# Row sums of an expert pair in one block, descriptor scratch cut to a quarter, and three quarters of weight unit 9 loaded into the place freed

## The chip, the cores and the metric

One core of one Trainium2 chip. The metric is the device time of one execution of the whole program in microseconds; where several executions are shown, their median counts. Profiles are of one execution; times in them are microseconds from the first instruction.

## The reference

One inference step of a one-layer encoder for a prompt of 512 rows and a sample of 32, model width 1024: an input projection `w_in` (8464 columns), an RWKV-7 branch and a chunked GLA branch, a gated merge, and a mixture of 32 experts (4 groups of 8, each token in the two best of its best group). The change is in the expert stage, and in what is loaded ahead of it:

```python
combine = jnp.sum(jax.nn.one_hot(expert_ids, N_EXPERTS, dtype=f32) * w_top[..., None], axis=1)
for e in range(N_EXPERTS):                       # D_MODEL 1024, EXPERT_FF 512, all float32
    hid = jax.nn.silu(ht @ e_gate[e]) * (ht @ e_up[e])
    out = out + combine[:, e:e + 1] * (hid @ e_down[e])
x = x + gt2 * out
y = _rmsnorm(x, final_norm_g)
```

Here `ht` are the normed rows of both streams, 544 in all, `gt2` a modulation from the condition `c` of the stream, and the outputs are `y` of both streams and the new states.

## The kernel before

The program has stages with their own semaphores and memory layout. The first makes the modulations and projects with `w_in` in 66 units of 128 columns; SyncE's queue loads them into two slots (L433), each load after the split of the unit two before (`w_split`). Beside the units 20 to 45 the GLA branch is computed for five tiles of rows. GpSimd (POOL) issues some DMAs in this stage: the GLA state (L513), and after each tile a store of its result `y_g` (`keep_y`, L521 to L525), each behind a wait on `y_g_out`, which VectorE raises twice per tile (L1162). VectorE waits for the five stores (`y_g_kept`) before it writes over that memory. The second stage is the recurrence. The third projects both branches with `w_branch_gla` and `w_branch_rwkv` in 16 units, called branches here: SyncE loads branch u + 2 (`load_branch`) once branch u is split (`wb_split`), and its gate rows (`load_gates`); ScalarE makes the high part of the weights (L1361, after the projection before the last is done), VectorE the rest (L1367), and TensorE multiplies (L2836). ScalarE's queue loads `w_out` and the residual rows beside branches 8 to 13. `gate_up_in` says that the small matrix `rwkv_gate_up` has landed. After a short output projection and the router comes the expert stage.

**The expert stage.** Experts are worked off in pairs p = 0 to 15, each expert for a block of up to 64 rows. The weights of an expert are three units of 2048 KB: gate, up, down. `STREAM` lists them per pair as gate 2p, up 2p, gate 2p+1, up 2p+1, down 2p, down 2p+1, so unit 9 is `up` 3. They go through a ring of eight slots (`RING`, `SLOT_AT`; one unit, `BESIDE`, has its own place). SyncE issues the loads in order (`load_unit`, L2155 to L2167; the DMA is at L2159 for whole units and at L2166 for quarters). A unit's slot is that of the ring unit eight before it; SyncE waits for TensorE to have read that one: `gu_mm` for a gate/up product, `dn_mm` for a down projection. Units 1 to 19 (`IN_QUARTERS`) are loaded in four quarters, each after the same quarter of the one before was read (`part_read`). `landed` tells the semaphore value for which TensorE waits.

Within a pair TensorE does, in order (L3131 to L3138):

- `gate_up(2p)`: for each of 8 slices k of the width, gate and up of the even expert into one bank (L3017). I call it product 2p. Before slice 6 it does `rows_added` of the pair before for tiles 0 and 1.
- `gate_up(2p+1)`: the same for the odd expert. Before slice 3 it turns the even product (`turned`, L3028) and does `rows_added` for tiles 2 and 3.
- `rows_turned(p+1)`: transposes the gathered rows of the next pair (L2991); `turned(2p+1)`.
- `rows_added(p-1, 4)`: the fifth tile.
- `down(p)`: both down projections (L3041), after VectorE's hidden rows (`hid_done`).

`rows_added(p, j)` (L3048 to L3063) brings the pair's results back to the places of their rows: a one-hot matrix times the result in two parts, 4 matmuls of 512 columns (L3061), into `ADD_BANKS[j]`: tiles 0 and 2 share banks 4 and 5, tiles 1 and 3 banks 6 and 7, tile 4 has banks 0 and 1, where the even product lies. VectorE adds each sum to the residual `x2` (`rows_summed`, L3529) and raises `moe_added`; the product for tile 2 waits for the sum of tile 0, that of tile 3 for tile 1. Banks 6 and 7 also take the turned rows, so `rows_turned` waits for the sum of tile 3, and `down` for that of tile 2. VectorE also copies products out (L3471), multiplies the hidden rows (L3464, after ScalarE's silu, L2704), scales the down result (L3497) and makes its two parts (ScalarE L2709, VectorE L3499). The last pair is done in another order (`held_rows`, `tile_so_far`, `last_rows`), and isn't touched.

POOL gathers the rows of the next pair with an indirect DMA (L2279) as soon as those of the present one are turned.

## Time and profile before

| | us |
|---|---|
| three runs | 1420.49, 1412.27, 1420.85 |
| median | 1420.49 |
| the profiled execution | 1418.71 |
| span of its trace | 1417.0 |
| TensorE busy in it | 1340.1 |
| VectorE, ScalarE, POOL busy | 704.2, 465.6, 173.3 |
| moved by DMA | 310.79 MB |

The span runs from the first to the last instruction; the execution's own time is 1.71 us longer. In the views PE is TensorE's matmuls, PEld its weight loads, DVE VectorE, ACT ScalarE, SPq and ACTq the DMA queues of SyncE and ScalarE. A wait stands behind the instruction that waited, as time and releaser. A DMA's landing is counted from its issue. "issue" is a wait for nothing that the profile shows. Matmuls are pipelined, so that the start of the next one tells more than the duration of one.

### The profile page before, as it was taken

Reading aid. Unit: us, or ns where it says so; the run is one execution under the profiler, and the core shown is the slowest. Engines: PE = TensorE matmul, PEld = TensorE weight load, DVE = VectorE, ACT = ScalarE, POOL = GpSimd, SP = SyncE. Lnnn points to the kernel's source line nnn. Section 1 sums busy time; section 2 is a strip of 40 time slices with the busy share of each in tenths; the row PEclk is TensorE's granted clock in tenths of the full one; section 3 lists DMA queues with packets and bytes.
Section 4 is the critical chain, followed back from the end, with each engine's and each line's share of the span. In section 5 each row is a group of like instructions: output and inputs, shape, how many; then the busy total and the mean of one; then the engine's idle time right before and its main releaser. Section 6 shows DMA issues by size and latency. Waiting matters only on the chain.

```text
span 1417.0 us, 30562 instructions
## 1 busy us (share of the span) xinstructions
PE 1340.1 (95%) x13401; PEld 986.4 (70%) x13401; DVE 704.2 (50%) x1139; ACT 465.6 (33%) x732; POOL 173.3 (12%) x212
## 2 busy tenths in 40 slices
PE   5899999999999997888889999999999999999997
PEld 1688899999999996777778998863444444343343
DVE  3413234553236556555576658634455544454454
ACT  2424235555665663343344343211100010000113
POOL 2000000000112213433430201000000000000000
PEclk9999999999999998999999999999999999999999
DMA  8566522224532210000052392899999999999993
GB/s 323 183 218 219 168 77 75 75 83 139 160 106 76 75 46 26 4 5 5 20 152 77 97 312 93 322 407 408 409 428 426 427 426 427 426 427 427 426 428 147
DMA packets 132932, 310.79 MB, mean 219 GB/s; under 512 B 13315, under 2 KB 98537, under 8 KB 119865
## 3 DMA queue, kind: packets, MB, share of 16 engines
q1 hardware_dynamic: 122078, 285.86, 53.9%
q10 hardware_dynamic: 7546, 15.58, 3.1%
q0 software_dynamic: 3168, 7.33, 1.4%
q8 instruction: 109, 1.79, 0.6%
q14 instruction: 31, 0.25, 0.1%
HBM read 299.88 MB, written 12.79 MB: 221 GB/s over the span
## 4 chain that ended last, share of the span: by engine, by line
PE 48%; DMA 7%; DVE 3%; issue 2%; ACT 1%; POOL 0%; SPq 0%; DVEq 0%; POOLq 0%; ACTq 0%
PE bank L3017 13%; PE bank L2836 7%; PE bank L3041 6%; DMA lower<-in_expert_w_up 4%; PE bank L3061 4%; PE bank L2864 3%; DMA upper7b<-in_expert_w_up 2%; PE bank L1761 2%; PE bank L1717 1%; PE bank L3028 1%; PE bank L2991 1%; PE bank L1818 1%; PE bank L1806 1%; PE bank L1793 1%; PE bank L2791 1%
## 5 line engine op out<-in xcount | busy, mean ns | idle before, releaser
L838 PE MATMUL bank<-upper2end 128*128 128x272 f32 x3168 | 416.7, 291 | 6.0 <-DVE upper2end L1065 5.4
L838 PEld LDWEIGHTS bank<-upper2end 128*128 128x128 f32 x3168 | 402.8, 189 | 26.9 <-issue 25.3
L3017 PE MATMUL bank<-upper7b 128*64 128x512 f32 x784 | 230.7, 596 | 7.6 <-issue 3.9
L1042 DVE TENSOR_TENSOR upper2end<-upper,upper2end 128x1024 fp32r<-128x1024 f32 x66 | 83.4, 1264 | 262.1 <-ACT upper2end L604 262.0
L3017 PEld LDWEIGHTS bank<-upper7b 128*64 128x64 f32 x784 | 69.8, 137 | 116.8 <-issue 116.5
L3017 PE MATMUL bank<-lower,upper7b 128*64 128x512 f32 x240 | 108.5, 596 | 2.4 <-issue 1.0
L3041 PE MATMUL bank<-upper7b,lower 128*64 128x512 f32 x352 | 106.3, 595 | 0.9 <-DVE lower L3464 0.9
L2836 PE MATMUL bank<-upper_r 128*128 128x272 f32 (+2 forms) x768 | 105.1, 293 | 0.0
L3529 DVE TENSOR_TENSOR lower<-lower,bank 128x1024 f32<-128x1024 f32 (+1 forms) x70 | 82.8, 1216 | 44.7 <-PE bank L3061 42.1
L2704 ACT ACTIVATE lower<-bank 128x256 f32<-128x256 f32 x32 | 12.3, 384 | 273.4 <-PE bank L3028 273.4
L2836 PEld LDWEIGHTS bank<-upper_r 128*128 128x128 f32 x768 | 98.2, 188 | 4.4 <-issue 0.9
L3061 PE MATMUL bank<-upper_r7b 128*128 128x512 f32 x280 | 75.3, 407 | 1.2 <-DVE upper_r7b L3499 1.2
L604 ACT ACTIVATE upper2end<-upper 128x1024 fp32r<-128x1024 f32 x66 | 69.6, 1054 | 17.0 <-DMA upper<-in_w_in 11.0
L3041 PEld LDWEIGHTS bank<-upper7b,lower 128*64 128x64 f32 x352 | 32.3, 137 | 49.4 <-issue 44.0
L2279 POOL DMA_INDIRECT lower<-expert_in,lower x16 | 16.0, 1000 | 398.5 <-PE bank L2991 388.4
L3061 PEld LDWEIGHTS bank<-upper_r7b 128*128 128x128 f32 x280 | 49.7, 190 | 21.2 <-issue 10.5
L2709 ACT ACTIVATE upper_r7b<-lower 128x1024 fp32r<-128x1024 f32 x15 | 15.9, 1057 | 127.3 <-DVE lower L3497 127.3
L3017 PEld LDWEIGHTS bank<-lower,upper7b 128*64 128x64 f32 x240 | 31.1, 137 | 33.2 <-issue 33.2
L3041 PE MATMUL bank<-lower 128*64 128x512 f32 x120 | 53.2, 595 | 0.0
L3471 DVE COPY lower<-bank 128x512 f32<-128x512 f32 x32 | 22.1, 692 | 60.9 <-PE bank L3017 60.9
L2864 PE MATMUL bank<-upper_r 128*128 128x512 f32 x192 | 45.8, 395 | 0.0
L1489 ACT ACTIVATE upper<-bank 128x512 f32<-128x512 f32 x36 | 21.5, 597 | 72.2 <-DVE upper L1574 72.0
(445 smaller groups left out, 1861.4 us busy)
## 6 DMA issues: line engine op xcount, KB each, us to landing
upper7b<-in_expert_w_gate SPq DMA_DIRECT2D x20, 2048.0 KB, 23.0
upper7b<-in_expert_w_up SPq DMA_DIRECT2D x19, 2048.0 KB, 28.3
upper7b<-in_expert_w_down SPq DMA_DIRECT2D x19, 2048.0 KB, 24.2
upper<-in_w_in SPq DMA_DIRECT2D x66, 512.0 KB, 3.9
lower<-in_w_ada SPq DMA_DIRECT2D x23, 1024.0 KB, 5.1
lower<-in_expert_w_down SPq DMA_DIRECT2D x7, 2048.0 KB, 25.0
lower<-in_expert_w_gate SPq DMA_DIRECT2D x6, 2048.0 KB, 21.9
lower<-in_expert_w_up SPq DMA_DIRECT2D x6, 2048.0 KB, 28.6
```

The costliest lines, as they stand in the source:

```text
L604: nc.scalar.activation(w_high[u % 2], w_slot[u % 2], ACT.Copy).then_inc(w_high_done, 1)
L838: m = mm(psum[s][:, c, 0:HALF], w_part[s][:, k, :], h_part[:, k, c * HALF:(c + 1) * HALF], start=k == 0 and w_part is w_high and h_part is ...
L1042: ve.tensor_tensor(w_rest[u % 2], w_slot[u % 2], w_high[u % 2].bitcast(F32), ALU.subtract).then_inc(w_split, 1)
L1489: nc.scalar.activation(kbv[c % 2][:, 2 * u:2 * u + 2].rearrange("p q h n -> p h q n"), psum[u % 2].rearrange("p h (q n) -> p h q n", n=256 ...
L1761: m = mm(out[r, j], lhs, pp[k % 2][r, j], start=True, stop=True)
L2836: m = mm(out, w[s][:, k, :], rhs, start=k == 0 and w is wb_high and y == "high", stop=k == KD - 1 and w is wb_rest)
L2864: m = mm(psum[OUT_BANKS[i]][:, 1 - b, :], m_part[side][:, k, t], w, start=k == first_k and m_part is m_high and w is not wo_rest[b][k], st ...
L3017: m = nc.tensor.matmul(GU_BANK[s][64 * b:64 * b + 64, :], x_t[:, k, s * BLK:(s + 1) * BLK], w[:, k, :], start=k == 0, stop=k == KD - 1)
L3041: m = nc.tensor.matmul(psum[2][64 * s:64 * s + 64, b, :], hid[s][:, f, :], down_rows(2 * p + s, f)[:, b * 512:(b + 1) * 512], start=f == 0 ...
L3061: m = nc.tensor.matmul(out[:, b, :], oh_t[:, j * P:(j + 1) * P], y_parts[part][:, b * 512:(b + 1) * 512], start=part == 0, stop=part == 1)
L3471: ve.tensor_copy(gu[e % 2], GU_BANK[e % 2]).then_inc(gu_out, 1)
L3529: ve.tensor_tensor(x2[0:n, j, :], x2[0:n, j, :], psum[ADD_BANKS[j]][0:n].rearrange("t b c -> t (b c)"), ALU.add).then_inc(moe_added, 1)
```

## The change

Four things. The scratch for POOL's descriptors is set to 4096 bytes, which leaves 12 KB per partition for a new tensor `apart`. Three quarters of unit 9 (`up` 3, slices 0 to 5) are loaded there, in three DMAs ahead of the load of branch 12, and TensorE reads these slices from there; only the last quarter still goes through the ring. The GLA state and the five stores of `y_g` are issued by SyncE instead of POOL, at units 22 and 28, 32, 36, 40, 44. And the five `rows_added` of a pair stand in one block in the odd product, before slice 3, in the order of tiles 0, 1, 4, 2, 3; VectorE's five sums likewise, after the hidden rows of the even expert.

```diff
+        apart = ctx.enter_context(nc.sbuf_tensor("apart", [P, 3 * D], F32)).rearrange("p (q k f) -> p q k f", q=3, k=2)
...
                 for u, (kind, f, col) in enumerate(UNITS):
+                    if u == 22:
+                        sp.wait_ge(b_sum, 2 * NG)
+                        sp.dma_start(st_g[1], I["state_gla"][0, 0].rearrange("h k v -> k h v")).then_inc(st_g_in, 16)
+                    if 28 <= u <= 44 and u % 4 == 0:
+                        i = (u - 28) // 4
+                        t0, wt = i * P, TILES[i][1]
+                        sp.wait_ge(y_g_out, 2 * i + 2)
+                        sp.dma_start(yg_dram[:, :, t0:t0 + wt].rearrange("n p t -> p n t"), y_g[:, :, t0:t0 + wt]
+                                     ).then_inc(y_g_kept, 16)
                     if u >= 2:
                         sp.wait_ge(w_split, u - 1)
...
-                pool.dma_start(st_g[1], I["state_gla"][0, 0].rearrange("h k v -> k h v")).then_inc(st_g_in, 16)
...
                     pool.tensor_tensor(q_st[:, :, 0:w], qk[:, 0:4, t], e_b[:, :, 0:w], ALU.mult).then_inc(q_st_done, 1)
-                    if i:
-                        keep_y(i - 1)
-                keep_y(4)
+                pool.wait_ge(y_g_out, 10)
...
-        gate_up_in = sem("gate_up_in", lasting=True)
+        apart_in = sem("apart_in", lasting=True)
...
+        APART = unit_no["up", 3]
...
         def parts_of(n):
-            return 4 if n in IN_QUARTERS else 1
+            return 4 if n in IN_QUARTERS and n != APART else 1
+        def load_apart(sp):
+            for q in range(3):
+                sp.dma_start(apart[:, q], eup[3][:, 2 * q:2 * q + 2]).then_inc(apart_in, 16)
+        def apart_landed(r):
+            return apart_in, r * 48 + 64
+        def block_rows(kind, e, k):
+            if unit_no[kind, e] == APART and k < 6:
+                return apart[:, k // 2, k % 2]
+            return weights_of(kind, e)[:, k, :]
...
+        ADD_ORDER = (0, 1, 4, 2, 3)
+        ADD_NO = {j: ADD_ORDER.index(j) + 1 for j in range(5)}
...
                 for u in range(NB):
+                    if u == 10:
+                        sp.wait_ge(apart_in, 16)
+                        load_apart(sp)
                     if u + 2 < NB:
                         sp.wait_ge(wb_split, u + 1)
                         load_branch(sp, u + 2)
...
                             for n in units:
-                                load_unit(sp, n, [q])
+                                if n != APART or q == 3:
+                                    load_unit(sp, n, [q])
...
                         if h == 0 and p >= 2:
-                            pe.wait_ge(moe_added, r * ADDS + (5 * p - 6))
+                            pe.wait_ge(moe_added, r * ADDS + (5 * (p - 2) + ADD_NO[3]))
...
+                    if unit_no["up", e] == APART:
+                        pe.wait_ge(*apart_landed(r))
...
-                        if s == 0 and k == 6 and 0 < p < P_LAST:
-                            rows_added(r, p - 1, 0)
-                            rows_added(r, p - 1, 1)
                         if s == 1 and k == 3:
                             turned(r, e - 1)
                             if 0 < p < P_LAST:
-                                rows_added(r, p - 1, 2)
-                                rows_added(r, p - 1, 3)
+                                for j in ADD_ORDER:
+                                    rows_added(r, p - 1, j)
...
                     if p:
-                        pe.wait_ge(moe_added, r * ADDS + (5 * p - 2))
+                        pe.wait_ge(moe_added, r * ADDS + (5 * (p - 1) + ADD_NO[2]))
...
                     if j in (2, 3):
-                        pe.wait_ge(moe_added, r * ADDS + (5 * p + j - 1))
+                        pe.wait_ge(moe_added, r * ADDS + (5 * p + ADD_NO[j - 2]))
...
                         turned(r, 2 * p + 1)
-                        if p:
-                            rows_added(r, p - 1, 4)
                         down(r, p)
...
                     for p in range(P_LAST):
-                        if p:
-                            rows_summed(r, p - 1, 0)
-                            rows_summed(r, p - 1, 1)
                         gate_up_copied(r, 2 * p)
                         hidden(r, 2 * p)
                         if p:
-                            rows_summed(r, p - 1, 2)
-                            rows_summed(r, p - 1, 3)
+                            for j in ADD_ORDER:
+                                rows_summed(r, p - 1, j)
                         gate_up_copied(r, 2 * p + 1)
                         rows_copied(r, p + 1)
                         hidden(r, 2 * p + 1)
-                        if p:
-                            rows_summed(r, p - 1, 4)
...
-    nc = bacc.Bacc("TRN2", target_bir_lowering=False, num_devices=1)
+    nc = bacc.Bacc("TRN2", target_bir_lowering=False, num_devices=1, dynamic_dma_scratch_size=4096)
```

## Rows read from the trace of the kernel before

**Rows 1.** The page: its first line.

```profile
span 1417.0 us, 30562 instructions
```

**Rows 2.** Busy time in stretches (us; engines; granted clock, DMA share, GB/s) of the expert stage.

```profile
939.00:956.00 17.00, 16.34 (x81) 6.42 (x80) 3.38 (x7) 0.77 (x2) 1.28 (x2) 1.00 1.03 408
985.00:1013.00 28.00, 28.00 (x133) 11.88 (x132) 14.03 (x17) 2.71 (x4) 0.99 (x1) 1.00 1.02 413
1242.00:1273.00 31.00, 29.00 (x135) 12.39 (x133) 14.53 (x17) 2.88 (x5) 1.35 (x2) 1.00 1.01 428
```

**Rows 3.** Chain that ended last, window 1190 to 1300 (start us, us, what).

```profile
1199.65 30.36 DMA lower<-in_expert_w_up
1291.52 2.80 PE bank L3017 x12
```

**Rows 4.** The same chain, window 800 to 1417.

```profile
985.74 7.09 PE bank L3041 x32
1321.39 30.54 DMA lower<-in_expert_w_up
1352.18 2.80 PE bank L3017 x12
```

**Rows 5.** Timeline of pair 7; last line: product 30. [idle before <-releaser].

```profile
1138.86 2.14 PE L3061 MATMUL bank<-upper_r7b 128*128 128x512 f32 x8
1140.92 4.51 PE L3017 MATMUL bank<-upper7b 128*64 128x512 f32 x20
1145.87 2.09 PE L3061 MATMUL bank<-upper_r7b 128*128 128x512 f32 x8
1147.08 2.35 DVE L3529 TENSOR_TENSOR lower<-lower,bank 128x1024 f32<-128x1024 f32 x2
1147.89 4.51 PE L3017 MATMUL bank<-upper7b 128*64 128x512 f32 x20
1152.33 1.16 PE L2991 MATMUL bank<-lower 128*128 128x128 f32 x8
1153.73 1.17 PE L3061 MATMUL bank<-upper_r7b 128*128 128x512 f32 x4
1154.35 0.99 POOL L2279 DMA_INDIRECT lower<-expert_in,lower  x1 [27.23 <-PE bank L2991]
1154.91 0.13 PEld L3041 LDWEIGHTS bank<-upper7b,lower 128*64 128x64 f32 x1 [0.43 <-DVE lower L3464]
1371.71 7.09 PE L3017 MATMUL bank<-upper7b 128*64 128x512 f32 x32 [0.17 <-issue]
```

**Rows 6.** DMA issues at 909.5, 1001.9, 1011.5, 1351.6 (count, KB, us to landing).

```profile
upper7b<-in_expert_w_up SPq DMA_DIRECT2D x1, 512.0 KB, 3.5
upper7b<-in_expert_w_gate SPq DMA_DIRECT2D x1, 2048.0 KB, 8.9
upper7b<-in_expert_w_down SPq DMA_DIRECT2D x1, 2048.0 KB, 9.8
upper7b<-in_expert_w_up SPq DMA_DIRECT2D x1, 2048.0 KB, 29.7
```

**Rows 7.** Waits by engine, 930 to 1417 (us, times, longest).

```profile
PE bank L3061 <- DVE upper_r7b L3499: 1.2, 1, 1.2
```

**Rows 8.** Branch stage: ScalarE's timeline, then the DMA issues at 818.5 and 836.6.

```profile
828.19 1.06 ACT L1361 ACTIVATE upper_r<-mid 128x1024 fp32r<-128x1024 f32 x1 [2.72 <-PE bank L2836]
846.27 1.06 ACT L1361 ACTIVATE upper_r<-mid 128x1024 fp32r<-128x1024 f32 x1 [1.41 <-PE bank L2836]
...
mid<-in_w_branch_rwkv SPq DMA_DIRECT2D x1, 512.0 KB, 6.6
mid<-in_w_branch_rwkv SPq DMA_DIRECT2D x1, 512.0 KB, 7.5
```

**Rows 9.** Timeline of VectorE and of SyncE's queue near unit 44.

```profile
361.82 0.60 DVE L1162 SCALAR_TENSOR_TENSOR lower<-bank,lower 128x128 f32<-128x128 f32 x2
...
365.27 0.37 SPq L433 DMA_DIRECT2D upper<-in_w_in  x1
```

More of the change, by code:

```diff
@@ L519, in _ @@
                 pool.wait_ge(pads, 5)
-                def keep_y(i):
-                    t0, wt = i * P, TILES[i][1]
-                    pool.wait_ge(y_g_out, 2 * i + 2)
-                    pool.dma_start(yg_dram[:, :, t0:t0 + wt].rearrange("n p t -> p n t"), y_g[:, :, t0:t0 + wt]
-                                   ).then_inc(y_g_kept, 16)
                 for i, w, nc_ in GLA_TILES:
@@ L1414, in recurrence_sync @@
             sp.wait_ge(s_mm, NCK)
-            sp.dma_start(rw_gate_up, I["rwkv_gate_up"][0]).then_inc(gate_up_in, 16)
+            sp.dma_start(rw_gate_up, I["rwkv_gate_up"][0]).then_inc(apart_in, 16)
             for s, out in ((0, O[3]), (1, O[6])):
@@ L2150, in parts_read @@
             return r * (9 * READ_PAIRS) + (9 * (e // 2) + (6 if kind == "down" else 3 * (e % 2)) + q + 1)
+        APART = unit_no["up", 3]
+        assert ring_no[APART] == 8
         def parts_of(n):
-            return 4 if n in IN_QUARTERS else 1
+            return 4 if n in IN_QUARTERS and n != APART else 1
[8 more added lines that the diff above has]
+            return weights_of(kind, e)[:, k, :]
         def load_unit(sp, n, quarters=range(4)):
@@ L2413, in a_round @@
                         sp.sem_inc(held, 1)
+                        load_apart(sp)
                         for n in range(9):
@@ L2794, in norm_gate @@
                 def norm_gate(k):
-                    pe.wait_ge(gate_up_in, 16)
+                    pe.wait_ge(apart_in, 16)
                     if k < 2:
@@ L3003, in gate_up @@
                             pe.wait_ge(moe_added, r * ADDS + (5 * p - 5))
-                    gate_and_up = weights_of("gate", e), weights_of("up", e)
                     for k in range(KD):
@@ L3013, in gate_up @@
                             if 0 < p < P_LAST:
-                                rows_added(r, p - 1, 2)
-                                rows_added(r, p - 1, 3)
-                        for b, w in enumerate(gate_and_up):
+                                for j in ADD_ORDER:
+                                    rows_added(r, p - 1, j)
+                        for b, kind in enumerate(("gate", "up")):
                             m = nc.tensor.matmul(GU_BANK[s][64 * b:64 * b + 64, :], x_t[:, k, s * BLK:(s + 1) * BLK],
-                                                 w[:, k, :], start=k == 0, stop=k == KD - 1)
+                                                 block_rows(kind, e, k), start=k == 0, stop=k == KD - 1)
                         if p < READ_PAIRS and k in (1, 3, 5):
@@ L3527, in rows_summed @@
                     n = TILES[j][1]
-                    v.wait_ge(moe_mm, r * ADDS + (5 * p + j + 1))
+                    v.wait_ge(moe_mm, r * ADDS + (5 * p + ADD_NO[j]))
                     ve.tensor_tensor(x2[0:n, j, :], x2[0:n, j, :],
```

## The prediction

> **What bounds the kernel now.** I read the page first: the span is 1417.0 us [rows 1], and the expert stage is its last third. Then the busy time by stretches of that stage. In the first pairs (939 to 956 us) and in the later ones (1242 to 1273 us) the DMA share is full; the rate is 408 GB/s where units come in quarters, 413 while that changes, and 428 where they come whole. TensorE is busy all the 28.00 us of 985 to 1013, but only 29.00 of the 31.00 us from 1242 on [rows 2]. So there are two regimes, and the chain of waits shows where one goes over into the other. It runs on TensorE alone from pair 1 (its down projection starts at 985.74) to 1199 us, and then goes through the transfers of odd `up` units: 30.36 us from 1199.65 into an odd gate/up product, and so in each second pair: TensorE starts such a product (12 matmuls before the turn) at 1291.52 and at 1352.18 [rows 3, 4]. That is 60.66 us for two pairs, 30.33 each. In the first regime the down projection of pair 7 starts at 1154.91, six pairs after 985.74: 28.2 us each [rows 4, 5]. The stream stays ahead of TensorE until about pair 9; from there TensorE waits some 2.1 us in each pair. The last such wait ends at 1352.18; what follows to the end is TensorE's own work, 64.8 us. **The end is therefore the landing of `up` 29 plus a tail of TensorE.** Both are touched by the change: the first by the bytes taken out, the second by the new place of the row sums.
>
> **Bytes taken out of the stream.** Three of four quarters of unit 9 (`up` 3) go: 3 x 512 KB = 1.573 MB. They belong to the stretch that runs at 408 GB/s [rows 2]: 1.573/408 = 3.85 us (3.7 at 428). The stream gives this on only if it never runs dry, since a transfer can't start before its place is free. Whether it does is told by the landing times of single issues. A quarter issued at 909.5, with little before it, lands after 3.5 us; a whole unit has 1.573 MB more, 3.7 us at 428, so one alone would take about 7.2 us (estimate from these two). At 1001.9 a unit took 8.9 us and one at 1011.5 took 9.8 [rows 6]: only 1.7 and 2.6 us of other work stood before them. That is less than 3.85, so the queue runs dry there unless TensorE frees these places sooner.
> The first it does free sooner. Before, product 4 held the first two row sums (8 matmuls, 1140.92 - 1138.86 = 2.06 us in the pair of rows 5), which leave it, and in pair 1 TensorE waited 1.2 us before these sums for the rounded rows [rows 5, 7], which it no longer needs there. So its place is free 1.2 + 2.06 - 0.5 = 2.8 us before 1001.9 (0.5 is what pair 1 gets longer, worked out below), more than the 2.15 that lack, and nothing is lost. The second isn't: product 5 gets the block, so its end lies at 1011.5 - 1.2 + 2 x 0.5 (pairs 1 and 2), some 0.2 us sooner. The unit can land at 1011.3 + 7.2 = 1018.5 where before it landed at 1021.3. The advance of the stream is cut to 2.8 us. From then on queued work only grows until TensorE starves, so it isn't cut again. Bounds: 3.85 if the stream doesn't run dry at all, 1.1 if a lone unit takes the 8.9 us of the row at 1001.9. I take **2.8 us**, since the lone landing is built from the row nearest to an empty queue.
> The Trainium skill, "DMA: Bandwidth & Descriptors", section "Anatomy of one DMA", has 2.0 us plus the bytes at 436 GB/s for one DMA: an estimate of 6.8 us for a unit, so the advance would be 3.2 instead of 2.8. The rows of this case have no unit on an empty queue that could decide it.
>
> **The row sums in one block.** In a pair (rows 5 show pair 7) they stand in three places: 8 matmuls in the even product (2.06 us), 8 in the odd one after the turn (1147.89 - 1145.87 = 2.02), and 4 between the turn of the odd product and the down projection [rows 5]. Twenty in one place: in the group of 8 a matmul costs 1.72/8 = 0.215 us and going over and back 0.3, so 20 x 0.215 + 0.3 = 4.6 us. VectorE has to follow: its sums take 2.35/2 = 1.18 us and start 1.2 us after the block. The fifth product (tile 3) needs the second sum, done 3.56 us after the start of the block, and TensorE comes to it after 16 matmuls, 3.4. That is a wait of 0.1; five sums end 7.1 us after the start, before the copy of the odd product is due (4.6 + 4.4 = 9.0), and the rows' turn waits for all five, also at 9.0. Bounds for the block: 4.6 and 5.5 (each dependent product waiting for its sum by half a microsecond).
> The third group gives nothing back. It filled time in which TensorE waits for the hidden rows: from the turn of the next rows (1152.33) to the down projection (1154.91) are 2.58 us, and the end of it is a wait for VectorE's product of L3464, 0.43 us [rows 5]. Without the four matmuls that wait is some 0.9 us longer and the projection starts no sooner. A pair so costs - 2.06 - 2.02 + 4.6 = +0.5 us: 28.7 instead of 28.2. In the first regime that is paid out of TensorE's lead. It stays under the 30.33 us of the stream, so the regimes stay; pair 14 would be reached by TensorE alone near 1343, the weights come at 1349.
> What is paid at the end is the tail. Before, sums 0 and 1 of pair 13 ran ahead of product 29, in the shade of the transfer that it waits for. Now all stand behind it. From 1352.18 to the start of product 30 at 1371.71 are 19.53 us, 0.17 of it a wait for weights, which goes: 19.36 + 4.6 - 2.02 = 21.94, **2.4 us more**. Bounds 1.5 (if the third group's 0.9 comes back after all) and 3.3 (the block at 5.5). Product 31's weights, issued at 1351.6, landed 29.7 us later [rows 6], at 1381.3, nearly ten after product 30 began, and would land earlier still, so they bind nothing in the tail.
>
> **The three quarters in the branch stage.** SyncE issues them right ahead of the load of branch 12, and they share the engines with w_out. They take 3.85 us of DMA. Branch 12's load, issued at 818.5, lands after 6.6 us (825.1), and ScalarE uses it at 828.19, after 2.72 us of waiting for TensorE: 3.1 us of room. Branch 15's, issued at 836.6, lands after 7.5 us (844.1) and is used at 846.27: 2.2 us [rows 8]. Behind that lies more room: a branch takes TensorE (846.27 - 828.19)/3 = 6.03 us, and the split of its weights 1.06 on ScalarE and about 1.2 on VectorE, with hand-overs some 2.5, so they may be 3.5 us late again. 3.85 us are covered by 5.7 at the tightest. Cost 0; without the cover it would be up to 3.85. Bounds 0 and 0.5 (the gate rows of branch 14 queue behind as well).
>
> **Moved DMAs.** The stores of y_g leave POOL's queue for SyncE's, each behind a wait on two VectorE products, and behind that wait stands the next w_in load. The tightest is the last: VectorE is through at 361.82 + 0.60 = 362.4, the load behind it went out at 365.27 anyway [rows 9]. The state's load, now at unit 22, waits for scans that by the code end at unit 13. The other four stores have the same pattern. Cost 0, bounds -0.5 and +0.5. The smaller scratch serves what POOL still issues, the gathers: POOL waited 27.23 us for TensorE before one of them [rows 5], so their descriptors have a pair's time: 0.
>
> **Sum.** -2.8 + 2.4 + 0 + 0 = -0.4 us. The profiled execution was 1418.71 us, 1.7 more than its span; it would be 1418.3. The three runs shown have a median of 1420.49, so the forecast for a median is 1420.49 - 0.4 = **1420.1 us**. Bounds of the terms: -3.85 + 1.5 - 0.5 = -2.85, and -1.1 + 3.3 + 1.0 = +3.2.
>
> **Rivals.**
> A. The whole gain: the stream doesn't run dry and the row sums cost nothing behind product 29, because the turned product and the sums hide there. -3.85: 1416.6. For it: the DMA share stays full everywhere in rows 2. Against: rows 6 show too little before the units of 1001.9 and 1011.5, and the tail is TensorE's throughout.
> B. Slower, by the tail: the block waits for VectorE's sums and the stream gives less than the tail takes. Place: between 1352 and 1371. Price +3.3, against an advance of 1.1: +2.2, 1422.7. It decides from the point where the advance is smaller than what the block adds behind product 29. For it: the fifth product reaches its sum within 0.1 us. Against: the five sums start in the same order as the products.
> C. The quarters collide in the branch stage. If three pieces don't overlap but take 3.5 us each [rows 6], they hold the queue for 10.5 us; beyond 5.7 us of room TensorE starts branch 15 4.8 us late: +4.4 with the rest, 1424.9. Against: quarters in a row run at 408 GB/s in rows 2, which is three in 3.85.
> By the Trainium skill, "DMA: Bandwidth & Descriptors", section "Bandwidth", DMAs under 1 MiB lose much of the peak. That is C's mechanism; the 408 GB/s of rows 2 for 512 KB pieces disagree with it as long as several are queued.
> D. The transfer leaves the stream and the end doesn't notice at all (another wait takes over at pair 14): +2.4, 1422.9. Against: the same transfer stands in the chain at 1199.65 and at 1321.39 [rows 3, 4].
>
> **How the numbers follow.** The forecast has 0.5, A 0.22, B 0.18, C 0.05, D 0.05. All lie within 5 us, while the three runs of the kernel before lie between 1412.27 and 1420.85, so the range is made as much by runs as by cases: from a low run less the forecast's gain and a little (1411.3) to B and D (1423.0). A change of over 1% is 14.2 us, about what a measurement of this kernel can tell from none. No case reaches it: TensorE never waits more than about 12 us in the whole stage (5.8 pairs by 2.1 us), and nothing added is worth more than 11. I leave 0.03 on each side for what I haven't seen.
>
> **What would show it.** In the changed kernel's trace: the chain still goes through an `up` unit into product 29, which starts at about 1349.4; the stretch from there to product 30 is 21.9 us; a pair in the first regime takes 28.7; the unit freed after product 5 lands after about 7 us, and the DMA share dips near 1012; TensorE waits 1.3 us or so for L3464 ahead of each down projection; branch 12 to 15 start as before. The prediction is wrong if the start of product 29 moves by less than 1 us or by all of 3.8, if the block takes over 5.5 us, or if TensorE no longer waits for weights at all.

## The result, and the profile after

| | before | after |
|---|---|---|
| median, us | 1420.47 (20 runs, 1412.27 to 1425.5) | 1424.9 (20 runs, 1421.04 to 1428.75) |
| the profiled execution | 1418.71 | 1428.57 |
| its span | 1417.0 | 1426.8 |

The ratio of the medians is 1.0031 with an interval of 1.0021 to 1.0042: slower by 3 to 6 us. One execution of e9 below took 2179.15 us at a mean granted clock of 0.56, where the others lie between 0.94 and 0.99; it is left out of e9's ratio. Forecast were 1420.1 us and a range of 1411.3 to 1423.0; the time lies above it. The median is that of rival C, to which the prediction gave 0.05, and the profile shows the loss in C's place, the branch stage, though not all of its 4.4 us.

First the chain that ended last, in the branch stage. Before, it ran on TensorE alone from 815 to 861 us. After (start us, us, what):

```profile
814.89 8.31 PE bank L2862 x66
...
825.63 13.30 DMA mid<-in_w_branch_rwkv
838.93 0.02 issue
838.95 1.07 ACT upper_r L1362
840.02 0.02 issue
840.04 0.04 DVE upper_r L1368
840.08 1.11 issue
841.18 0.72 DVE mid L3254
841.91 0.14 issue
842.04 24.37 PE bank L2862 x192
```

Branch 12's load, 6.6 us before [rows 8], takes 13.3 and is in the chain. ScalarE's timeline shows what comes of it; compare the 2.72 us of waiting for TensorE in rows 8, which was the room:

```profile
829.31 1.06 ACT L1362 ACTIVATE upper_r<-mid 128x1024 fp32r<-128x1024 f32 x1 [4.96 <-PE bank L2862]
829.33 0.38 ACTq L2665 DMA_DIRECT2D lower<-in_w_out  x1
832.99 2.01 ACT L2593 ACTIVATE upper_r<-lower 128x1024 fp32r<-128x1024 f32 x2 [2.62 <-DMA lower<-in_w_out]
838.95 1.06 ACT L1362 ACTIVATE upper_r<-mid 128x1024 fp32r<-128x1024 f32 x1 [3.94 <-DMA mid<-in_w_branch_rwkv]
...
851.04 1.06 ACT L1362 ACTIVATE upper_r<-mid 128x1024 fp32r<-128x1024 f32 x1 [4.56 <-DMA mid<-in_w_branch_rwkv]
```

Branch 12 starts 838.95 - 829.31 = 9.64 us after branch 11, instead of 6.02. The queue of SyncE has the cause: the three quarters ahead of the load, and an issue of gate rows that itself takes 3.9 us instead of 0.58 (it stands behind the load and doesn't delay it).

```profile
821.48 1.43 SPq L2162 DMA_DIRECT2D apart<-in_expert_w_up  x3
825.63 0.38 SPq L1343 DMA_DIRECT2D mid<-in_w_branch_rwkv  x1
826.05 3.90 SPq L1346 DMA_DIRECT2D mid<-gates  x1
```

The expert stage in the chain after, from pair 0 on (the down projection that ends pair 1 stands at 994.68, as 985.74 did in rows 4):

```profile
965.96 7.09 PE bank L3065 x32
...
994.68 7.09 PE bank L3065 x32
...
1023.44 7.09 PE bank L3065 x32
...
1329.08 31.05 DMA lower<-in_expert_w_up
1360.37 2.79 PE bank L3041 x12
1363.17 0.68 PE bank L3052 x4
1363.85 4.61 PE bank L3085 x20
1368.46 4.44 PE bank L3041 x20
1372.90 1.09 PE bank L3017 x8
1375.41 7.09 PE bank L3065 x32
1382.50 6.87 PE bank L3041 x32
```

Here the prediction's reading held: the block of 20 matmuls takes 4.61 us, a pair takes 28.76 us from one down projection to the next (1023.44 - 994.68), and the chain still comes through an odd `up` unit into product 29. From there to product 30 are 21.96 us; its first matmul starts at 1382.33 in the timeline, while the chain books it at 1382.50. Among the waits of the expert stage is now the one that the third group of row sums used to fill. It stands ahead of each down projection (total us, times, longest):

```profile
PE bank L3065 <- DVE lower L3486: 13.9, 15, 0.9
```

And the unit freed after product 5, issued at 1021.0, lands later than I had it (8.1 us against 7.2). The DMA share around that moment dips, as forecast (us; engines; granted clock, DMA share, GB/s):

```profile
upper7b<-in_expert_w_down SPq DMA_DIRECT2D x1, 2048.0 KB, 8.1
```

```profile
966.00:995.00 29.00, 28.07 (x134) 12.47 (x136) 14.67 (x18) 4.01 (x5) 1.26 (x2) 1.00 1.01 391
1008.00:1024.00 16.00, 15.07 (x76) 8.05 (x74) 9.80 (x12) 0.77 (x2) 0.99 (x1) 1.00 0.88 342
```

The two profiled executions differ by 9.9 us, twice what the medians do. Stage by stage (my sums of starts in the two traces): the recurrence +5.0, branches 0 to 11 +1.2, branch 11 to the first expert product (product 0) +2.6, product 0 to 29 -1.5, 29 to 31 +2.4, the rest +0.2. The first two lie ahead of everything that the change could touch in that stage; I come back to the first. The second has its explanation in the same trace: TensorE's granted clock was at its lower level, 1.2 GHz, for 3.4 us from 742.0, and again for 3.4 us from 926.3, which is behind the first w_out product. The kernel before has 1.00 from 727 to 939 us.

```profile
742.00:745.40 3.40, 3.01 (x14) 2.73 (x15) 3.30 (x6) 2.60 (x5) 0.00 (x0) 0.50 0.40 103
926.30:929.70 3.40, 3.40 (x14) 2.94 (x13) 2.98 (x17) 0.60 (x1) 0.95 (x1) 0.50 1.02 405
```

The stretch with the first takes 96.65 us instead of 95.37, and the one with the second (first w_out product to product 0) 82.3 instead of 80.8. So 1.5 of the 2.6 us from branch 11 to product 0 lie behind the branch stage; in the branch stage itself it is 1.05.

### The profile page after: what moved, and what is told of

Its sections match the earlier page's. It is cut to its first block, busy times and chain, and to the rows that moved or that the text cites. A ratio compares the mean times of both kernels' runs of the same rounds, so it can differ in the third digit from the quotient of the medians.

```text
span 1426.8 us, 30563 instructions
## 1 busy us (share of the span) xinstructions
PE 1342.1 (94%) x13401; PEld 996.4 (70%) x13401; DVE 704.2 (49%) x1139; ACT 465.9 (33%) x732; POOL 169.5 (12%) x206
## 4 chain that ended last, share of the span: by engine, by line
PE 48%; DMA 6%; DVE 4%; issue 2%; ACT 1%; POOL 0%; DVEq 0%; SPq 0%; POOLq 0%; ACTq 0%
PE bank L3041 14%; PE bank L3065 6%; PE bank L2862 6%; PE bank L3085 4%; PE bank L2890 3%; DMA upper7b<-in_expert_w_up 2%; DMA lower<-in_expert_w_up 2%; PE bank L1718 1%; PE bank L1762 1%; PE bank L3052 1%; PE bank L3017 1%; DMA mid<-in_w_branch_rwkv 1%; PE bank L1819 1%; PE bank L1807 1%; PE bank L1794 1%
## 5 line engine op out<-in xcount | busy, mean ns | idle before, releaser
L3041 PE MATMUL bank<-upper7b 128*64 128x512 f32 x772 | 221.8, 594 | 5.0 <-DMA upper7b<-in_expert_w_up 3.4
L3085 PE MATMUL bank<-upper_r7b 128*128 128x512 f32 x280 | 67.7, 396 | 0.0
L3519 DVE TENSOR_TENSOR lower<-bank,lower 128x1024 f32<-128x1024 f32 x15 | 18.4, 1225 | 66.8 <-PE bank L3065 66.7
```

The costliest lines, as they stand in the source:

```text
L3041: m = nc.tensor.matmul(GU_BANK[s][64 * b:64 * b + 64, :], x_t[:, k, s * BLK:(s + 1) * BLK], block_rows(kind, e, k), start=k == 0, stop=k = ...
L3085: m = nc.tensor.matmul(out[:, b, :], oh_t[:, j * P:(j + 1) * P], y_parts[part][:, b * 512:(b + 1) * 512], start=part == 0, stop=part == 1)
L3519: ve.tensor_tensor(y_full, psum[2].rearrange("t b c -> t (b c)"), coef, ALU.mult).then_inc(y_done, 1)
```

## The experiments

From each trace I take four stretches: **R**, the recurrence (ScalarE's last split of `w_in` to its first branch); **B**, from branch 11 on ScalarE to product 0; **S**, from product 0 to product 29; **T**, from product 29 to 31. Ratios are against runs of the kernel before that were taken beside each kernel on the same chip (medians 1419.36 to 1420.48). A ratio and its interval are estimated from all these runs and aren't the quotient of the medians; for e13 the two differ most (1.0006 and 1.0019). The stretches are of one trace each, from starts in its chain, which lie up to 0.1 us behind the first matmul where TensorE runs without a gap.

| kernel | median | ratio [interval] | R | B | S | T |
|---|---|---|---|---|---|---|
| before | 1420.47 | | 199.1 | 116.8 | 413.2 | 30.4 |
| after | 1424.9 | 1.0031 [1.0021, 1.0042] | 204.1 | 119.4 | 411.7 | 32.8 |
| e1 block only | 1422.03 | 1.0012 [1.0003, 1.0022] | 200.6 | 116.9 | 411.8 | 32.8 |
| e2 no block | 1425.11 | 1.0027 [1.0005, 1.0049] | 200.7 | 120.4 | 412.3 | 30.4 |
| e3 space only | 1419.88 | 1.0000 [0.9986, 1.0014] | 196.0 | 118.9 | 412.5 | 30.4 |
| e4 quiet load | 1420.13 | 0.9993 [0.9974, 1.0012] | 196.8 | 117.0 | 411.3 | 32.8 |
| e5 late unit | 1416.39 | 0.9977 [0.9962, 0.9992] | 198.5 | 116.8 | 408.3 | 30.4 |
| e6 late unit, block in pair 1 | 1413.6 | 0.9957 [0.9942, 0.9972] | 198.6 | 116.9 | 408.9 | 30.6 |
| e7 quiet load, no block | 1418.48 | 0.9993 [0.9977, 1.0009] | 197.3 | 117.2 | 412.3 | 30.4 |
| e8 collision only | 1424.03 | 1.0023 [1.0008, 1.0038] | 198.0 | 118.3 | 413.0 | 30.4 |
| e9 behind branch 12 | 1422.06 | 1.0016 [1.0001, 1.0032] | 200.2 | 118.1 | 412.2 | 30.5 |
| e10 one quarter | 1420.31 | 1.0008 [0.9994, 1.0023] | 195.5 | 117.1 | 412.4 | 30.6 |
| e13 idle place | 1422.0 | 1.0006 [0.9991, 1.0021] | 204.0 | 117.2 | 412.1 | 30.4 |

### Taking the change apart

**e1**, the row sums in one block and nothing else of the change:

```diff
-                                rows_added(r, p - 1, 2)
-                                rows_added(r, p - 1, 3)
+                                for j in ADD_ORDER:
+                                    rows_added(r, p - 1, j)
```

> The kernel before with nothing of the change but the row sums in one block. Theory T (the block puts about 2.6 us behind the last awaited weights, the transfer gives back about 1.5, its collision in the branch stage costs about 1, the rest of the difference is where the clock was granted): product 29 starts at the same distance from product 0 as before (413.1 us), product 30 22.1 us after it instead of 19.5, a pair takes 28.75 us, the time is 2 to 3 us over the kernel before. Rival R (the moved DMAs, the smaller scratch or the new tensor slow the first stages): this one, which has none of them, is 0 to 1 us over the kernel before. Rival Q (the block hides, most is the collision): within 0.5 us of before.

**e2**, the changed kernel with the row sums back in their three places (the diff above turned round).

> The changed kernel with the row sums where they were. T: branch 12 still waits for its weights, about 1 us lost in the branch stage; product 29 comes 1 to 1.5 us sooner after product 0 than 413.1; product 30 19.5 us after it; the time is that of the kernel before within 1 us, so 3 to 4 us under the changed kernel. R: still 3 to 4 us over the kernel before. Q: about 4 us over before.

**e3**, the scratch of 4096 bytes, the moved stores and the tensor `apart`, but nothing is loaded there:

```diff
-                        sp.wait_ge(apart_in, 16)
-                        load_apart(sp)
```

> Smaller scratch, the tensor apart reserved but neither loaded nor read, and the stores of y_g and the state load on SyncE's queue; row sums and weight loads as in the kernel before. T: within 1 us of the kernel before, no stage changed. R: 3 to 4 us over, lost before the branch stage, in the recurrence above all. Q: within 1 us.

**e4**, the changed kernel with the three quarters loaded six branches earlier, where the DMA engines have room (their share is 0.29 from 760 to 780 us in the kernel before):

```diff
-                    if u == 10:
+                    if u == 4:
                         sp.wait_ge(apart_in, 16)
                         load_apart(sp)
```

> The changed kernel, but the three quarters are loaded before branch 6's weights instead of branch 12's, where the engines are idle more than half the time. T: no branch waits for its weights, some 1 us under the changed kernel. R: the same as the changed kernel. Q: 4 us under the changed kernel.

These four give the picture. Space and moved stores cost nothing (1.0000). The block alone costs 1.6 us (1422.03 against 1420.48), and its trace says how: product 29 comes 1 us earlier and T is 2.3 longer. The wait of rows 7 in pair 1 is gone in that trace, but that this is what brings product 29 forward isn't shown; e6 below speaks against it. Without the block the kernel isn't faster, so the block isn't the main loss. And e4, which moves nothing but one place of issue, is back at 1420.13. The theory that I had written down before these runs (T: the block costs most, the collision about 1 us) missed e2 and e4; Q, for which the collision is most of the loss, came out nearer in both; e1 lies between the two. e4's branches run through, in the chain that ended last, as before:

```profile
814.96 43.94 PE bank L2862 x350
```

### The collision by itself

**e8**, as e3, but the three quarters are loaded at branch 12 as in the change, as a surplus: the ring still loads all of `up` 3, TensorE reads it from there, and the loaded copy isn't used. So only the three DMAs are added to the branch stage.

```diff
-        APART = unit_no["up", 3]
+        APART = None
```

> The kernel before with the small scratch, the moved DMAs and the three quarters loaded ahead of branch 12, but the ring still loads all of unit up 3 and TensorE reads it from there: the three loads are surplus, nothing of the stream changes, row sums in three places. Theory (the collision at branch 12 is the main loss of the change): branch 11 to 12 takes 9.6 to 9.9 us instead of 6.0, with 4 us of waiting for in_w_branch_rwkv, and the time is 1420.5 + 4 = 1424.5, ratio 1.003. Rival 1 (the collision costs only what the branch stage as a whole shows, branch 11 to the first w_out product 1 to 2 us longer): 1422, ratio 1.001. Rival 2 (it is hidden): 1420.5, ratio 1.000.

1424.03, ratio 1.0023, which is 1.1 to 5.4 us: three surplus loads cost, as far as the runs can tell, most of what the whole change loses. The profiled execution, of 1418.62 us, was one of its fastest, so its trace can't show the whole of that. In the chain it is the same 13 us:

```profile
817.29 13.18 DMA mid<-in_w_branch_rwkv
830.47 0.02 issue
830.49 1.07 ACT upper_r L1362
```

**e10**: two quarters ahead of branch 6, one ahead of branch 12, no block.

```diff
+                    if u == 4:
+                        load_apart(sp, (0, 1))
+                    if u == 10:
+                        load_apart(sp, (2,))
```

> Same kernel with two quarters ahead of branch 6 and one ahead of branch 12: a third of the collision. Branch 12's load lands some 2.2 us later than before (a third of the 6.7 it was late behind three), inside the 3 us of room: branch 12 still 6.0 to 6.2 us after branch 11, and the time as without a collision, 1418.5 to 1420, ratio 0.9993. If the cost goes with the bytes: a third of 4 to 5 us, 1420.5, ratio 1.0003.

ScalarE still waits for TensorE ahead of branch 12, but only half as long:

```profile
829.10 1.06 ACT L1362 ACTIVATE upper_r<-mid 128x1024 fp32r<-128x1024 f32 x1 [1.47 <-PE bank L2862]
```

In the kernels with no quarter there the same wait is 2.6 to 3.1 us. Branch 12's load landed 7.65 us after its issue instead of 6.6: one quarter takes 1.1 us out of the room and costs nothing in the trace (B 117.1). Three take 6.7, more than three times as much. The ratio of 1.0008 doesn't tell 0 from a third of the cost.

**e9**: all three issued behind branch 12's load, no block.

```diff
                     if u + 2 < NB:
                         sp.wait_ge(wb_split, u + 1)
                         load_branch(sp, u + 2)
+                    if u == 10:
+                        sp.wait_ge(apart_in, 16)
+                        load_apart(sp)
```

> As the kernel with the row sums in their three places and the three quarters at branch 12, but the three loads issued behind branch 12's load instead of ahead of it. Theory 1 (the loss is that branch 12's own load queues behind them on SyncE's queue): branch 12 comes 6.0 us after branch 11 as before; branch 13's load is issued some 6 us later, when most of the quarters are through, so it has room; 1419 to 1420, ratio 0.9995. Theory 2 (the loss is the DMA engines' capacity beside w_out and the residual rows, which were at a share of 1.0 from 820 to 845 before): the wait only moves to branch 13 or to the w_out pieces, the branch stage stays 1 to 2 us longer and the time is 1423 to 1425, ratio 1.002 to 1.003.

The wait moves to branch 13:

```profile
831.45 1.06 ACT L1362 ACTIVATE upper_r<-mid 128x1024 fp32r<-128x1024 f32 x1 [3.07 <-PE bank L2860]
831.47 0.38 ACTq L2663 DMA_DIRECT2D lower<-in_w_out  x1
840.14 1.06 ACT L1362 ACTIVATE upper_r<-mid 128x1024 fp32r<-128x1024 f32 x1 [5.73 <-DMA mid<-in_w_branch_rwkv]
```

It is 2.7 us late (840.14 - 831.45 = 8.69 against 6.02), and all of that is made good before the first w_out product (36.07 us from branch 11, before 35.99). So this order of issue moves the wait and doesn't remove it. The run time is up 2 us all the same, with an interval that nearly reaches 1; and the trace has no more than 0.8 in B for it (118.1 against the 117.3 that the quiet kernels, those whose branches aren't late, have on average).

**e13**: the three loads behind the last branch, near 856 us, where the DMA share falls off; no block.

```diff
                 sp.wait_ge(wb_split, NB)
                 sp.dma_start(gt1_b[1], mod_dram[1, 2 * D:3 * D].partition_broadcast(P)).then_inc(gt1_in, 16)
+                sp.wait_ge(apart_in, 16)
+                load_apart(sp)
```

> Unit up 3 as in the change, row sums in three places, but the three loads issued after the last branch is split and behind the first modulation row, near 849 us, where the DMA share of the kernel before was 0.22 and falling. Theory (it is the collision with the branch weights, w_out and the residual rows that costs): nothing is late, branch 11 to product 0 about 117 us, time as with the load ahead of branch 6, 1418.5 to 1420, ratio 0.999 to 1.000. Rival (any late place costs, for instance by waking the DMA engines in the quiet stretch or by making the modulation rows of 861 to 865 us late): branch 11 to product 0 over 118.5 and 1422 or more, ratio 1.0015.

Nothing is late in the trace: B 117.2. The ratio of 1.0006 (-1.3 to +3.0 us) takes in 1, but the median of 1422.0 is above what was expected and is the one that the rival had. By the trace a late place isn't bad in itself, while a full one is; the times don't settle it.

### What the early unit gives, and what a late one would

**e7**: as e4, without the block.

> Unit up 3 as in the change, its three quarters loaded ahead of branch 6 instead of branch 12, row sums in their three old places. Theory: the advance of the early unit shrinks on the dry queue to 0.5 to 1 us; product 29 comes 0.5 to 1 us earlier (466.5 to 467.0 from the first expert load), nothing is paid behind it; branch 12 starts 6.0 us after branch 11; time 1419.8, ratio 0.9995. Rival (the full 2.8 us of the prediction arrive when no block is there): 464.7 and 1417.7, ratio 0.998.

S is 412.3. The six kernels with the quarters of `up` 3 apart and no block (e2 and its repetition, e7, e9, e10, e13) have 412.1 to 412.4, mean 412.3; the four without them and without the block (before, e3, e8 and its repetition) 412.5 to 413.2, mean 412.8. The 3.85 us of transfer taken out give **0.5 us**, a small difference of two groups whose nearest traces are 0.1 apart.

**e5**: as e7, but it is `up` 15 whose three quarters lie apart:

```diff
-        APART = unit_no["up", 3]
+        APART_E = 15
+        APART = unit_no["up", APART_E]
...
-                sp.dma_start(apart[:, q], eup[3][:, 2 * q:2 * q + 2]).then_inc(apart_in, 16)
+                sp.dma_start(apart[:, q], eup[APART_E][:, 2 * q:2 * q + 2]).then_inc(apart_in, 16)
...
             if n not in IN_QUARTERS:
+                if n == APART:
+                    sp.dma_start(weights_of(kind, e)[:, 6:8], source[e][:, 6:8]).then_inc(unit_in[sem_of(n)], 16)
+                    return
```

> Row sums in their three old places, three quarters loaded ahead of branch 6 (where they disturbed nothing), but of unit up 15, which is needed late in the stage, when the stream is far from running dry; its fourth quarter goes through the stream. Theory (the gain of the bytes was lost because the queue ran dry behind the early unit): the stream reaches product 29 by 1.573 MB / 428 = 3.7 us earlier than before, counted from the first expert load (before 467.5, so 463.8), nothing is paid behind it, and the time is 1420.5 - 3.7 = 1416.8, ratio 0.9974. Rival (the end does not follow the bytes, something else takes over): product 29 where it was, 1420.5, ratio 1.000.

1416.39, ratio 0.9977 (1.1 to 5.4 us faster): the same number of bytes in the same place of the memory, and S falls by 4.5 us to 408.3, in one trace. The chain of e5 reaches product 29 through a landing as before, and no block stands behind it:

```profile
1318.08 30.44 DMA lower<-in_expert_w_up
1348.77 2.79 PE bank L3045 x12
1352.24 1.84 PE bank L3089 x8
```

**e6**: as e5, with the block in pair 1 alone:

```diff
+                                for j in ADD_ORDER if p == 1 else (2, 3):
```

> As the kernel with up 15, and the five row sums in one block in pair 1 alone; the later pairs keep their three places. Theory: the wait of 1.2 us in pair 1 goes and the tail pays nothing, so product 29 comes a further 1.3 us earlier if that stall reached it through the places freed later (462.5 from the first expert load), and the stretch from product 29 to 31 stays 30.4. Time 1415.5, ratio 0.9965. Rival: the stall of pair 1 is swallowed by the queued work as long as the stream is ahead; then it is as the kernel without the block, 1416.8.

1413.6, ratio 0.9957: better than both kernels, by 6 us (interval 4 to 8) than before. But its step isn't shown. The stall of pair 1 is gone in the trace, S isn't shorter than in e5 (408.9 against 408.3), as the rival has it, and the intervals of e5 and e6 overlap. What the runs show is the late unit.

### Traces again: is there more than the collision?

The quiet kernels had a shorter R than the colliding ones up to here, though R is over before the quarters are issued. So I took further traces: **e11** and **e12** are e2 and e8 once more, **e14** and **e16** the changed kernel, **e15** and **e17** e4, each with the kernel as it was. e17 ran on another chip, where one run of the kernel before took 1425.02.

> The kernel with the three quarters at branch 12 and the row sums in three places once more, for a second trace. Theory (a late branch 12 costs 1 to 2 us there, and the rest of the 4 to 5 us sits elsewhere): branch 11 to 12 9.5 to 9.9 us again, and a further stretch before product 0 is longer than the 80.8 us from the first w_out product to product 0 (82.4 in the first trace, with a granted clock of 0.83 for 20 us). Rival: that stretch was chance (the kernel with the space alone had 82.9 without a collision); then it is 80.8 here.

> The collision alone once more, for a second trace; its first trace was one of its three fastest runs (1418.6 at a median of 1424.0), so it cannot show where the median loses. Theory: branch 11 to 12 at 9.5 us again, and in a run near its median some 3 to 4 us more than in the first trace, in the branch stage from 11 to the first w_out product (38.0 us or more instead of 36.9) or in the stretch to product 0. Rival: the further time lies ahead of branch 12, in the recurrence (198 us in the first trace), where it has nothing to do with the load.

> The changed kernel once more, for a trace. Theory 1 (the place of the load acts on the recurrence too): recurrence 200 to 204 us. Theory 2 (chance): 196 to 200, as the others. From branch 11 to product 0 119 to 120.5 in either case.

> The changed kernel with the three quarters ahead of branch 6, once more, for a trace. Theory 1: recurrence 196 to 199 us. Theory 2 (chance): anything from 196 to 204. From branch 11 to product 0 117 in either case.

> The changed kernel a third time. As for the second: recurrence 200 to 204 by theory 1, anything from 196 to 204 by theory 2; branch 11 to product 0 119 to 120.5.

> The changed kernel with the three quarters ahead of branch 6 a third time. Recurrence 196 to 199 us if the place of the load acts on it, anything from 196 to 204 if it was chance; branch 11 to product 0 117.

| | time | R | branch 11 to w_out | w_out to product 0 | S | T |
|---|---|---|---|---|---|---|
| e11 (as e2) | 1426.4 | 203.2 | 38.2 | 82.5 | 412.3 | 30.4 |
| e12 (as e8) | 1423.81 | 199.9 | 37.4 | 82.7 | 412.6 | 30.4 |
| e14 (as after) | 1423.9 | 197.7 | 37.9 | 81.4 | 411.7 | 32.8 |
| e16 (as after) | 1425.22 | 201.1 | 38.0 | 81.1 | 411.6 | 32.8 |
| e15 (as e4) | 1421.12 | 202.4 | 36.0 | 81.3 | 411.7 | 32.8 |
| e17 (as e4) | 1420.41 | 199.1 | 36.0 | 82.8 | 411.4 | 32.8 |

R is 197.7 to 204.1 in the seven colliding traces (mean 200.7) and 195.5 to 204.0 in the eleven quiet ones (198.9; e10 counts among them, e9 in neither group): they overlap nearly whole, and the changed kernel alone covers 197.7 to 204.1. I take it for chance. The branch stage doesn't overlap: from branch 11 to the first w_out product 36.9 to 38.2 us (mean 37.7) where the quarters collide, 35.99 in all eleven where they don't: **1.7 us** more. The stretch behind it (mean 82.0 against 81.3) overlaps again; it is long where the granted clock fell near 925 us (below). B as a whole: 119.6 against 117.3, **2.3 us**, of which the 0.6 in that stretch aren't shown to come from the quarters.

## Why the prediction was wrong

**The three quarters in the branch stage: costed at 0 (bounds 0 to 0.5), measured 1.7 us in the branch stage and 2.3 in B.** This is the step that failed, and what took the time out of the range: e4, which differs only in their place, is back inside it. Two things in it were wrong. I took the price of the quarters from the expert stage, where 512 KB pieces run at 408 GB/s [rows 2], and never asked how full the DMA engines are here. One more view of the kernel before would have told (us; engines; granted clock, DMA share, GB/s):

```profile
817.00:847.00 30.00, 30.00 (x241) 30.00 (x240) 16.52 (x21) 13.09 (x15) 0.00 (x0) 1.00 1.03 330
```

For thirty microseconds the share is 1.03, at 330 GB/s: the transfers of `w_out`, of the residual rows, of branches and gate rows fill all 16 engines. Room at one load's landing is no room when the queue has none. And the quarters had the engines for themselves in my sum; in the changed kernel two queues share them, as the queue shares from 821.5 to 838.9 show (packets, MB, share of 16 engines; q1 holds SyncE's loads, by its bytes: three quarters, two branches and their gate rows are 3.2 MB; q10 ScalarE's pieces of `w_out`):

```profile
q1 hardware_dynamic: 3636, 3.61, 62.3%
q10 hardware_dynamic: 777, 2.99, 43.3%
```

At 62% of the engines the 1.573 MB ahead of branch 12's load take more than 1.573/408: the load lands 13.3 - 6.6 = 6.7 us later. Less the 3.1 us of room that is 3.6, and branch 12 is 9.64 - 6.02 = 3.6 us late. The "more room behind" of the prediction was there, in part: branch 12 is 3.5 to 3.8 us late in the seven traces, and 1.0 to 2.3 of that reach the first w_out product. The prediction let a branch be 3.5 us late before TensorE notices; here TensorE waited 0.7 to 1.0 us ahead of branch 12, by the profile for a gated product of VectorE (L3254), which stands behind the split of the late weights. ScalarE waits for branch 14's load again (4.56 us above). In the profiled execution that costs TensorE nothing, its only wait is the first line here, but in four of the seven traces it waits a second time, as in e14 (second and third line).

```profile
842.04 14.20 PE L2862 MATMUL bank<-upper_r 128*128 128x256 f32 x111 [0.78 <-DVE mid L3254]
...
836.75 12.27 PE L2862 MATMUL bank<-upper_r 128*128 128x256 f32 x96 [0.87 <-DVE mid L3254]
849.64 6.63 PE L2862 MATMUL bank<-upper_r 128*128 128x256 f32 x51 [0.62 <-DVE mid L3254]
```

C named this collision, and its figure of 10.5 us for three quarters is near: the last landed 10.8 us after its issue. But it had this from pieces that don't overlap, whereas they waited for loads ahead of them and shared the engines with `w_out`; the load behind them was 6.7 us later, and TensorE lost 1.7 us on average, not 4.8. That C's 1424.9 is the measured median is luck. That the rate of DMAs under 1 MiB is poor, the rule of the Trainium skill ("DMA: Bandwidth & Descriptors", section "Bandwidth"), doesn't show as the cause: in the first 1.7 us behind their issue the engines moved 414 to 433 GB/s, more than in rows 2's 408. Over the whole 17.4 us it was 380; what part the size of the pieces has in that isn't shown.

**Bytes taken out: costed at -2.8 (bounds -3.85 to -1.1), measured -0.5 by themselves and -1.2 with the block's own gain.** The measure is product 29 against product 0: 412.8 on average in the four traces with neither, 411.6 in the six with both. The steps up to the place freed after product 4 were right: counted from product 0, its unit lands at 67.8 us in e4 against 71.7 in e1, 3.9 ahead, and the next is also 3.95 ahead. Then the queue runs dry, as said, but the rest of the step is mis-sized. The unit after product 5 takes 7.9 to 8.2 us instead of my 7.2 (the estimate of 6.8 from the Trainium skill's "DMA: Bandwidth & Descriptors", section "Anatomy of one DMA", is further off; its fit is for DMAs that GpSimd issues, and these are SyncE's), so 2.0 us of the advance are left; and its neighbour, issued 0.4 us later, lands at 86.3 against 87.1: 0.75 left. From 72.6 to 86.3 e4 lands two units in 13.7 us, e1 from 76.6 to 87.1 in 10.5: the stream stood still for 3.2 us. I had followed the advance to the first landing after the gap and not to the second, which is the one that all later units queue behind. In e4's trace it stays at 0.8 to 0.9 us over the next units; in the changed kernel's own trace it is 0 by 117.7 us. At product 29 it is 0.3, between e1 (411.85) and the six (411.6).

**"From then on it isn't cut again"** and "the end follows the bytes" are borne out by e5: where the stream is deep, 1.573 MB give 4.5 us at product 29 (3.7 expected). Rival D's mechanism, another wait that takes over at pair 14, stands in no chain; but for unit 9 its outcome, that the end hardly notices, was nearer than mine: 0.5 us of 2.8.

**The row sums: +2.4 behind product 29, measured 2.35 by the starts of the chains (32.75 - 30.40), 2.33 by the first matmuls.** Block 4.57 to 4.61 us (4.6), pair 28.76 (28.7), the wait of 0.93 us ahead of the down projection, where I had 1.3. The gain ahead, which I put down to 1.2 us of stall in pair 1, is 1.0 in e1's S, with its cause open (e6); it was in the -2.8. Net the block costs 1.3 us by the traces, and e1 measures 1.6 (by its ratio 0.4 to 3.1).

**Moved stores, scratch: 0, measured 1.0000** (0.9986 to 1.0014).

**The sum as it should have been**, from traces: -1.2 + 2.3 + 2.3 = +3.4 us, or +2.8 with the 1.7 of the branch stage alone. The medians say +4.4, with an interval of 3.0 to 6.0. The same sum for e8 is +2.3 (by its ratio 1.1 to 5.4), for e4 +1.1 (by its ratio -3.7 to 1.7). What is left, 1 to 1.6 us, stays open: R is 1.8 us longer on average in the colliding kernels, which may be chance, and the traces can't settle it. The 2 us of e9, whose branch stage is as before, stay open too.

Rival A (the whole gain) did not occur. B was near on the advance (1.1, measured 1.2) and wrong on the block, which waits for no sum. The range was too narrow by the step costed at 0: its upper bound of 0.5 had been worked out from the room of one load, while the cost without cover, 3.85, stood in the text and was not let into it. Even the bounds as they stand add up to +3.2, 1423.7, and the range ended at 1423.0.

## What to carry to other kernels

Before a transfer is moved into another stage, read the DMA share of that stage, not the landing time of one load in it: at a share of 1.0 whatever is queued behind the new bytes lands later (here 1.1 us for one quarter, 6.7 for three), and the room behind has to cover that. Bytes taken out of a stream are worth their time only from the last point where the stream runs dry; the advance has to be followed through every gap, to the last of the units issued together after it, and the unit to take out is one that comes when the queue is deep (here `up` 15, 4.5 us, against `up` 3, 0.5). A place of issue is a free parameter: e4 differs from the changed kernel by one line.

## What the runs showed of the hardware

- The first of two 2 MB transfers on a queue that had run dry landed after 7.9 to 8.2 us, while in a full queue units land every 4.9 us (71.7 to 76.6 in e1). The second, issued 0.4 us later, landed 5.8 to 6.1 us behind the first (80.2 and 86.3 in e4), against 4.9 in e1 (82.2 and 87.1): the stream isn't back at its rate at once.
- An issue of gate rows held SyncE's queue for 3.8 to 5.1 us in the seven colliding traces, where it stood behind three quarters and branch 12's load, and for 0.58 us in the kernel before. Full engines alone don't do it: in the kernel before the DMA share was 1.03 in the same stretch. What does, isn't shown.
- One kernel's own executions spread over 8 to 14 us (the kernel before 13, the changed one 8, e4 14), and part of it is the granted clock. In the recurrence, where TensorE has gaps, the profiled executions differ: the first fence is before, the second after, both from 540 to 580 us.

```profile
540.00:580.00 40.00, 32.19 (x1194) 29.02 (x1196) 22.85 (x50) 12.55 (x22) 16.80 (x16) 0.87 0.05 11
```

```profile
540.00:580.00 40.00, 31.41 (x1023) 28.48 (x1026) 20.95 (x46) 11.46 (x20) 15.24 (x16) 0.74 0.06 17
```

At 0.74 of full speed, a mean over stretches at 2.4 and at 1.2 GHz, TensorE did 1023 matmuls instead of 1194 in the same 40 us. Over the whole of R the granted clock was 0.95 before and 0.91 after, and 0.97 in the shortest R (e10, 195.5 us). So the profiled execution of the changed kernel was 5 us longer in a stage that the change doesn't reach: compare stages of several traces before a difference of two spans is explained. The same dip appears near 925 us, behind the router (0.83 to 0.85 over 10 us), in five of the seven colliding traces and in two of the eleven quiet ones; whether a late branch brings it on isn't shown. It is what makes the stretch from the first w_out product to product 0 take 82.3 to 83.0 us in six of these seven traces, instead of 80.8 to 81.4 in the others, e9 (82.0) apart.
